# Splitting attention's operands for single-pass matmuls, with part of a convolution on GpSimd

## The reference

```python
def conformer_conv_branch(u, w_dw, b_dw, ln_g, ln_b, w_pw_out):
    a, gate = jnp.split(u, 2, axis=-1)
    h = a * jax.nn.sigmoid(gate)
    h = lax.conv_general_dilated(h, w_dw[:, None, :], window_strides=(1,),
        padding=[(15, 15)], dimension_numbers=("NWC", "WIO", "NWC"),
        feature_group_count=2048) + b_dw
    h = jax.nn.silu(layer_norm(h, ln_g, ln_b))
    return h @ w_pw_out
...
    s = (jnp.einsum('bqhd,bkhd->bhqk', qn, k_nope)      # 128 dims a head
         + jnp.einsum('bqhr,bkr->bhqk', qr, k_rope))    # 64 rotary dims
    p = jax.nn.softmax(s * scale, axis=-1)
    return jnp.einsum('bhqk,bkhd->bqhd', p, v)
```

## Time and profile before

| | |
|---|---|
| median of 3 runs | 2312.63 us (2312.46 to 2313.82) |
| the profiled execution | 2312.04 us |
| its span, first to last instruction | 2310.2 us |
| mean granted TensorE clock | 0.999 of full speed |
| PE / PEld / DVE / ACT busy | 2292.7 / 1919.1 / 1338.2 / 1182.7 us |
| DMA | 432.63 MB, mean 187 GB/s, queue busy for 60.9% |

### The profile page before, as it was taken

One profiled execution on the slowest core, in us unless ns is written; L12 is line 12 of the kernel. 1 busy time (PEld: TensorE's weight loads), 2 busy tenths in 40 slices (PEclk: granted clock), 3 DMA queues, 4 the chain that ended last, 5 costly groups with the idle time before them and its releaser, 6 DMA issues.

```text
span 2310.2 us, 26652 instructions
## 1 busy us (share of the span) xinstructions
PE 2292.7 (99%) x10658; PEld 1919.1 (83%) x10658; DVE 1338.2 (58%) x1482; ACT 1182.7 (51%) x1596; POOL 0.2 (0%) x4
## 2 busy tenths in 40 slices
PE   9999999999999999999999999999999999999998
PEld 7888888888888888878899988888888888888887
DVE  5545544544545488988875486555544544554444
ACT  6444444444444577787777554454444444444443
POOL 0000000000000000000000000000000000000000
PEclk9999999999999999999999999999999999999999
DMA  8666666666666666566644456656666666666664
GB/s 295 192 188 191 189 186 195 191 185 191 191 191 189 192 188 186 183 186 189 201 136 121 131 179 199 187 187 206 188 191 191 191 186 190 190 189 193 193 192 153
DMA packets 121739, 432.63 MB, mean 187 GB/s; under 512 B 13712, under 2 KB 14224, under 8 KB 121488
## 3 DMA queue, kind: packets, MB, share of 16 engines
q1 hardware_dynamic: 121472, 430.51, 60.9%
q10 hardware_dynamic: 144, 0.43, 0.0%
HBM read 428.78 MB, written 2.10 MB: 187 GB/s over the span
## 4 chain that ended last, share of the span: by engine, by line
PE 97%; DVE 1%; ACT 1%; issue 1%; DMA 0%; SPq 0%; ACTq 0%; DVEq 0%
PE bank L760 31%; PE bank L762 31%; PE bank L761 31%; PE turned L771 2%; PE bank L939 1%; PE bank L913 1%; PE bank L914 1%; DVE q_rope L1239 0%; PE turned L924 0%; DVE q_rope L1245 0%; DMA xt<-in_xt_in 0%; ACT w_hi L483 0%; DVE w_lo L1035 0%; ACT q_rope L610 0%; ACT opened L515 0%
## 5 line engine op out<-in xcount | busy, mean ns | idle before, releaser
L1035 DVE TENSOR_TENSOR w_lo<-raw,w_hi 128x1024 fp32r<-128x1024 f32 x811 | 983.1, 1215 | 931.6 <-ACT w_hi L483 931.2
L483 ACT ACTIVATE w_hi<-raw 128x1024 fp32r<-128x1024 f32 x811 | 849.8, 1051 | 990.0 <-PE bank L762 979.1
L760 PE MATMUL bank<-w_hi,h 128*128 128x512 f32 (+1 forms) x2132 | 830.6, 390 | 1.9 <-DVE w_lo L1035 1.9
L762 PE MATMUL bank<-w_hi,h 128*128 128x512 f32 (+1 forms) x2132 | 827.7, 388 | 0.0
L761 PE MATMUL bank<-w_lo,h 128*128 128x512 f32 (+1 forms) x2132 | 827.3, 388 | 0.0
L760 PEld LDWEIGHTS bank<-w_hi,h 128*128 128x128 f32 x2132 | 400.3, 188 | 84.0 <-DVE w_lo L1035 3.4
L762 PEld LDWEIGHTS bank<-w_hi,h 128*128 128x128 f32 x2132 | 400.2, 188 | 82.3
L761 PEld LDWEIGHTS bank<-w_lo,h 128*128 128x128 f32 x2132 | 400.4, 188 | 80.7
L760 PE MATMUL bank<-w_hi,hidden 128*128 128x512 f32 x704 | 274.4, 390 | 0.0
L762 PE MATMUL bank<-w_hi,hidden 128*128 128x512 f32 x704 | 274.1, 389 | 0.0
L761 PE MATMUL bank<-w_lo,hidden 128*128 128x512 f32 x704 | 274.0, 389 | 0.0
(11 more groups left out here) (201 smaller groups left out, 1251.9 us busy)
## 6 DMA issues: line engine op xcount, KB each, us to landing
raw<-in_ffn_up SPq DMA_DIRECT2D x349, 512.0 KB, 4.1
raw<-in_ffn_down SPq DMA_DIRECT2D x176, 512.0 KB, 3.6
raw<-in_conv_in SPq DMA_DIRECT2D x64, 512.0 KB, 3.7
raw<-in_conv_gate SPq DMA_DIRECT2D x32, 512.0 KB, 4.2
raw<-in_mla_gate SPq DMA_DIRECT2D x32, 512.0 KB, 4.2
raw<-in_mla_out SPq DMA_DIRECT2D x32, 512.0 KB, 3.6
raw<-in_conv_out SPq DMA_DIRECT2D x32, 512.0 KB, 3.6
raw<-in_w_out SPq DMA_DIRECT2D x32, 512.0 KB, 3.6
```

The costliest lines, as they stand in the source:

```text
L483: act.activation(w_hi[:, j, 0:n], raw[:, j, 0:n], ACT.Copy).then_inc(hi_ready, 1)
L760: pe.matmul(dst, fixed_hi, moving_hi, start=first, stop=False)
L762: return pe.matmul(dst, fixed_lo, moving_hi, start=False, stop=last)
L1035: dve.tensor_tensor(w_lo[:, j, 0:n], raw[:, j, 0:n], w_hi[:, j, 0:n], ALU.subtract).then_inc(lo_ready, 1)
```

## The change

**Attention.** `q_nope`, `k_nope`, `q_rope`, `k_rope`, the values and the turned probabilities are stored as float32r in two parts, hi and lo, and the three float32 products become calls of `multiply`. ScalarE writes each hi part out of the bank and VectorE subtracts to get each lo part; the queries' copy moves from VectorE to ScalarE. The lo parts' semaphores are what TensorE now waits for. In a step, on both engines, the copies of queries, keys and values now stand ahead of the unit's rounding and splitting.

**Convolution.** GpSimd computes tiles 12 to 15 alone, with 62 instructions of 128x1024, each waiting for the one before. ScalarE and VectorE keep three groups of 31 taps, spread at 0.72 of a tap for each unit from 286 to 340, 0.4 to 364, and 0.87 to 416, with none in the heads. The sums lie in a tensor of their own name, `scratch`, at the old place; the split operands lie over `h`, which is not read then.

```diff
-        k_rope = sb("k_rope", [P, 2, T])
-        q_nope = sb("q_nope", [P, 2, T])
-        k_nope = sb("k_nope", [P, 2, T])
-        value = sb("value", [P, 2, 2, 2 * P])
+        k_rope = sb("k_rope", [P, 2, 2, T], F32R)
+        value = sb("value", [P, 2, 2, 2 * P], F32R)
...
-        N_TAPS = 4 * TAPS
+
+        SPARE, GATES = plan.stage("latents")[1].u0 + 4, plan.at("conv_gate") + 12
+        N_TAPS = 3 * TAPS
+        POOL_DONE = 2 * TAPS
 
         def taps_due(u):
 
-            n = int(0.85 * max(0, min(u, QR0) - CONV0)) + max(0, u - H0 - 4)
+            n = int(0.72 * max(0, min(u, SPARE) - CONV0) + 0.4 * max(0, min(u, GATES) - SPARE)
+                    + 0.87 * max(0, min(u, QR0) - GATES))
...
             def attend_out(p):
                 act.wait_ge(value_summed, p + 1)
                 if p == 4:
                     act.wait_ge(tap_done, CONV_DONE)
+                if p == 0:
+                    act.wait_ge(pool_tap, POOL_DONE)
...
+            def keep_queries(s):
+                act.wait_ge(unit_used, H0 + 4 * s + 2)
+                if s:
+                    act.wait_ge(scores_ready, 2 * s)
+                act.activation(q_nope[:, :, 0, :], q_bank[:, :].rearrange("p (j t) -> p j t", j=2), ACT.Copy).then_inc(q_hi, 1)
...
+                if part == 1 and 0 <= s < PAIRS:
+                    keep_queries(s)
+                if part == 2 and 0 <= s < PAIRS:
+                    keep_keys(s)
+                if part == 3 and 0 <= s < PAIRS:
+                    keep_values(s)
                 if u < HALVED:
                     open_unit(u)
                 else:
...
-                        pe.matmul(dst, q_nope[:, j, cols], k_nope[:, j, :], start=True, stop=False)
-                        last = pe.matmul(dst, q_rope[:, p, 0, cols], k_rope[:, j, :], start=False, stop=True)
+                        multiply(dst, (q_nope[:, j, 0, cols], q_nope[:, j, 1, cols]),
+                                 (k_nope[:, j, 0, :], k_nope[:, j, 1, :]), True, False)
+                        last = multiply(dst, (q_rope[:, p, 0, cols], q_rope[:, p, 1, cols]),
+                                        (k_rope[:, j, 0, :], k_rope[:, j, 1, :]), False, True)
...
-                        last = pe.matmul(out_bank[:, j * T:(j + 1) * T], value[:, p % 2, k, j * P:(j + 1) * P],
-                                         probs_t[:, j, k * T:(k + 1) * T], start=(k == 0), stop=(k == 1))
+                        dims, keys = slice(j * P, (j + 1) * P), slice(k * T, (k + 1) * T)
+                        last = multiply(out_bank[:, j * T:(j + 1) * T],
+                                        (value[:, p % 2, k, dims], value_lo[:, p % 2, k, dims]),
+                                        (probs_t[:, j, keys], probs_lo[:, j, keys]), k == 0, k == 1)
...
+        @block.gpsimd
+        def _(pool):
+            g = plan.stage("conv_in")[7]
+            pool.wait_ge(small_loaded, 64)
+            pool.wait_ge(cleared, 2)
+            pool.wait_ge(turn_hi, turns[g.turn + 1].hi_before + 1)
+            m = slice(12, 16)
+            at = (P, 4, T)
+            pool.tensor_tensor(pool_acc, padded[:, m, 0:T], taps[:, m, 0:1].to_broadcast(at), ALU.mult).then_inc(pool_tap, 1)
+            pool.wait_ge(pool_tap, 1)
+            pool.tensor_tensor(pool_acc, pool_acc, taps[:, m, TAPS:TAPS + 1].to_broadcast(at), ALU.add).then_inc(pool_tap, 1)
+            for t in range(1, TAPS):
+                pool.wait_ge(pool_tap, 2 * t)
+                pool.tensor_tensor(pool_prod, padded[:, m, t:t + T], taps[:, m, t:t + 1].to_broadcast(at),
+                                   ALU.mult).then_inc(pool_tap, 1)
+                pool.wait_ge(pool_tap, 2 * t + 1)
+                dst = conv[:, m, :] if t == TAPS - 1 else pool_acc
+                pool.tensor_tensor(dst, pool_acc, pool_prod, ALU.add).then_inc(pool_tap, 1)
...
+            def attend_turn(p):
+                for j in range(2):
+                    n = plan.probs_turn + 2 * p + j
+                    dve.wait_ge(turn_hi, turns[n].hi_before + 1)
+                    dve.tensor_tensor(probs_lo[:, j, :], turned_bank[n % 2][:, :], probs_t[:, j, :],
+                                      ALU.subtract).then_inc(turn_lo, 1)
```

More of the change, by code:

```diff
@@ L184, in encoder @@
         x = sb("x", [P, 2, D])
-        h = sb("h", [P, KT, 2, T], F32R)
+        outs = ExitStack()
+        h = sb("h", [P, KT, 2, T], F32R, outs)
+        outs.close()
+        outs = ExitStack()
+        q_rope = sb("q_rope", [P, PAIRS, 2, T], F32R, outs)
+        q_nope = sb("q_nope", [P, 2, 2, T], F32R, outs)
+        k_nope = sb("k_nope", [P, 2, 2, T], F32R, outs)
+        probs_lo = sb("probs_lo", [P, 2, 2 * T], F32R, outs)
+        value_lo = sb("value_lo", [P, 2, 2, 2 * P], F32R, outs)
+        outs.close()
+        sb("place_of_h", [P, KT, 2, T], F32R)
         identity = sb("identity", [P, P])
@@ L325, in encoder @@
         tap_done = sem("tap_done")
+        pool_tap = sem("pool_tap")
         key_step = sem("key_step")
         query_step = sem("query_step")
+        q_hi = sem("q_hi")
+        k_hi = sem("k_hi")
+        v_hi = sem("v_hi")
         q_copied = sem("q_copied")
@@ L585, in take_late_turns @@
                     rows = slice(ROPE * j, ROPE * (j + 1))
-                    act.activation(k_rope[rows, j, :], t[rows, 0:T], ACT.Copy).then_inc(turn_hi, 1)
+                    act.activation(k_rope[rows, j, 0, :], t[rows, 0:T], ACT.Copy).then_inc(turn_hi, 1)
             def make_tap(n):
@@ L1176, in take_turns @@
                     k = 2 * b + (0 if g.kind in ("kv", "q1") else 4 * g.i)
-                    if g.kind in ("up", "merge"):
-                        dst = hidden if g.kind == "up" else merged
+                    if g.kind in ("up", "merge", "qrope"):
+                        dst = {"up": hidden, "merge": merged, "qrope": q_rope}[g.kind]
                         dve.wait_ge(turn_hi, t.hi_before + 1)
@@ L1195, in take_late_turns @@
                                              op1=ALU.subtract).then_inc(turn_lo, 1)
+                dve.wait_ge(turn_hi, turns[plan.k_turn].hi_before + 2)
+                for j in range(2):
+                    rows = slice(ROPE * j, ROPE * (j + 1))
+                    dve.tensor_tensor(k_rope[rows, j, 1, :], turned_bank[plan.k_turn % 2][rows, 0:T], k_rope[rows, j, 0, :],
+                                      ALU.subtract).then_inc(turn_lo, 1)
             def clear_once():
@@ L1262, in keep_queries, with keep_keys, keep_values @@
             def keep_queries(s):
[L1263 to L1267, removed]
+                dve.wait_ge(q_hi, s + 1)
+                dve.tensor_tensor(q_nope[:, :, 1, :], q_bank[:, :].rearrange("p (j t) -> p j t", j=2), q_nope[:, :, 0, :],
+                                  ALU.subtract).then_inc(q_copied, 1)
+            def keep_keys(s):
+                dve.wait_ge(k_hi, s + 1)
+                dve.tensor_tensor(k_nope[:, :, 1, :], k_bank[:, :].rearrange("p (j t) -> p j t", j=2), k_nope[:, :, 0, :],
+                                  ALU.subtract).then_inc(k_copied, 1)
+            def keep_values(s):
+                dve.wait_ge(v_hi, s + 1)
+                hi, lo = (v[:, s % 2, :, :].rearrange("p k d -> p (k d)") for v in (value, value_lo))
+                dve.tensor_tensor(lo, v_bank[:, :], hi, ALU.subtract).then_inc(v_copied, 1)
+            def attend_turn(p):
+                for j in range(2):
+                    n = plan.probs_turn + 2 * p + j
+                    dve.wait_ge(turn_hi, turns[n].hi_before + 1)
+                    dve.tensor_tensor(probs_lo[:, j, :], turned_bank[n % 2][:, :], probs_t[:, j, :],
+                                      ALU.subtract).then_inc(turn_lo, 1)
             def split_heads(p):
@@ L1373, in _ @@
                     attend_inv(s - 1)
-                if part == 1 and 0 <= s < PAIRS:
-                    keep_queries(s)
                 if (s == PAIRS + 1 and part == 0) or (2 <= s <= PAIRS and part == 1):
                     split_heads(s - 2)
+                if part == 3 and 1 <= s <= PAIRS:
+                    attend_turn(s - 1)
                 if LN_SUMS <= u < LN_SUMS + 4:
```

39 lines of the change are left out of this document (17 added, 22 removed).

## The result

| | before | after |
|---|---|---|
| median | 2312.61 us (2312.46 to 2313.82, 4 runs) | 2402.45 us (2402.26 to 2403.39, 4 runs) |
| ratio | | 1.039, interval 1.0378 to 1.0402 |
| profiled execution, and its span | 2312.04 us, 2310.2 us | 2402.26 us, 2400.5 us |

The account below looks back on a forecast made before the run. TensorE, busy for 2292.7 of 2310.2 us, was taken to bound the kernel. From 2312.04 us, -7.0 - 2.6 - 1.9 + 0.5 = -11.0 gave 2301 us, with a range of 2297 to 2343.

Parts of the forecast that it names:

- 1. Fewer passes: Attention: three float32r matmuls replace each float32 one, saving 0.88 us a pair of heads, 7.0 us in 8 pairs.
- 2. The copies: Attention's added copies and subtractions on ScalarE and VectorE stay hidden except in the last pair: plus 0.5 us.
- the one tight place: Last pair of heads: the probabilities' lo part comes after TensorE is ready for the values, plus 0.5 us, between 0 and 1.
- 3. The waits of 2.6 and 1.9 us: With fewer taps, TensorE's waits before scores (2.6 us) and for late w_lo splits in the latents (1.9 us) go.
- 4. GpSimd: Convolution of tiles 12 to 15 on GpSimd, 924.5 to 1212.6 us: taken alone, costs nothing up to four times VectorE's price.
- the deadline: GpSimd's 62 instructions must end when the first heads' output is copied, 1212.6 us: 4.6 us for each.
- Rival A: From 924.5 to 1212 us VectorE and GpSimd exclude each other: 2319 to 2367 us, slower than before; chance 0.27.
- The bounds for p: Time of one GpSimd instruction, bounded by the same size elsewhere: 1.22 us on VectorE, 1.99 us on ScalarE.
- the term "- 57.5": VectorE's idle time, 46 us to 1170 us and 11.5 to 1212, subtracted from GpSimd's total time under mutual exclusion.
- Rivals B and C: GpSimd and VectorE slow each other a little, 2305 to 2316 us, chance 0.10; only half the gain, 2304 to 2308, 0.05.

Follow-up runs that it names:

- The spread version: The changed kernel with GpSimd's 62 instructions held back to lie evenly over TensorE's units up to 416, same result: 2369.12 us.
- attention's part alone: The changed kernel without GpSimd's block, all four convolution groups on ScalarE and VectorE at the old rates: 2316.58 us, ratio 1.0016 to the kernel before.

## Why the prediction was wrong

**1. Fewer passes: right.** The turns of consecutive pairs begin at 1295.77, 1311.03 and 1326.29 us in the changed kernel's chain:

```profile
1295.77 0.87 PE turned L952 x8
1311.03 0.87 PE turned L952 x8
1326.29 0.87 PE turned L952 x8
```

A pair lasts 15.26 us in place of 16.11: 0.85 us less, with 0.88 forecast; 6.8 us in eight pairs, with 7.0 forecast.

**2. The copies: right**, and the one tight place cost 0.2 us in place of 0.5. But the cover was worked out for heads without taps. The runs with taps there show how thin it is: 7.0 us of waits with one tap a unit.

**3. The waits of 2.6 and 1.9 us: right.** Both are gone once GpSimd is out (2301.12).

**4. GpSimd: here it failed.** The step says that the work, taken alone, is free up to four times VectorE's price. Unhindered it takes 1.97 us for a product and 2.40 for a sum, well under the 4.6 of the deadline, and its end came at 1088.6, well before 1212. But it isn't alone: the forecast put its cost to TensorE at nothing, which rested on the two engines running side by side. For the most part they don't, and it cost 101.3 us by the medians. Of the 101.6 between the two profiled executions, 99.1 are VectorE's delay and 2.5 the low granted clock behind it.

**Rival A was the case, and too weak in two ways.** First its chance. It got 0.27, with "against it: no row", though the lack of a row said nothing either way; VectorE's 85% said that the price would be high if it came. The Trainium skill (SBUF — State Buffer, section "Who interferes with whom") states the rule, and the runs bear out each half of it: two SBUF inputs against a GpSimd instruction that reads are shut out (2402), against one that only writes they are not (2302.6). A written rule that names the very kinds of instruction in the diff should have been the likeliest case, and the range should have reached it. Second its size. The bounds for p were 1.22 and 1.99, and p was 2.2 in the mean; the estimate of 2.25 from the Trainium skill (GPSIMD Engine Reference, section 3.1) was near it, and with it the rival said 2383. And the term "- 57.5" counted VectorE's idle time up to 1212 us. Taking turns, GpSimd forces its way through at once, so it had only the 12.4 us idle of the first 63.9. With 134.7 and 12.4 the rival's sum would be 2423, above what was measured, because it lets nothing run side by side. The 2383 is as near as it is since two errors work against each other. The spread version shows that the term's idle time is real if the work is held back: 43.0 us, and a loss of 68.0.

**Rivals B and C** were not the case. VectorE wasn't slowed evenly: beside GpSimd a split took 3.0 us in the mean and an instruction that reads PSUM its usual 0.47. And without GpSimd's work all of the gain was there.

## What to carry to other kernels

- Before elementwise work goes to GpSimd, look at what VectorE does at the same time. If its instructions read two SBUF tensors, most of GpSimd's reading work is added to its time and not put beside it. It is free only up to VectorE's idle time in the very stretch, and has to be spread out to find more (101 us lost in one row, 68 spread).
- Gain and cost of a joint change may come from different halves. Here one half was worth 7 us and the other cost 101; the good half kept most of its worth, 2305.2 us, once the convolution's taps were moved out of the heads by four numbers.

## What the runs showed of the hardware

- While a GpSimd instruction that reads SBUF runs, one of VectorE with two SBUF inputs stands still until shortly before its end, and the reverse: a split took 2.92 us in place of 1.22, four instructions of 0.48 took 9.19, and a sum on GpSimd 3.23 in place of 2.40.
- An instruction of VectorE that takes its data from PSUM isn't held by GpSimd. Its second input may even lie in SBUF. From the changed kernel's timeline, with a GpSimd sum from 1002.12 to 1005.38 us:

```profile
1003.05 1.65 DVE L1235 SCALAR_TENSOR_TENSOR c_kv<-turned,gains,c_kv 128x256 fp32r<-128x256 f32 x4
```

  These are four of 470 ns each, the next one starting before the last has ended in the records, where the kernel before has 466 ns.
- An instruction with one tensor input in SBUF can be held too, by reading and by writing: the scaling of `prod` (128x512) took 2284 ns beside GpSimd's arithmetic and up to 1250 beside its constant writes, in place of 484. Nor does a tiny size help: a scaling of 128x2 elements in SBUF (line 1121) has a median of 171 ns and took up to 2224 ns.
- Waits of TensorE cost more than their length once the granted clock falls: between 1190 and 1245 us of attention's part alone, 7.2 us of idle time brought it to 0.94 and 0.93. The kernel before, with 2.6 us idle in the same stretch, had 1.00. In the changed kernel it was 0.77 in the mean while GpSimd worked, between 1.00 from 925.8 to 940 us and 0.51 from 980 to 990. That cost little there, since VectorE set the pace (busy for 158.1 of 162.8 us); what showed were the 2.5 us behind it, where TensorE ran on at 0.50.
